# The next expert's gate products between an expert's up and down products, with its weights by whole rows and all programs written out

## The reference

```python
def ec_moe(h, lp):
    probs = jax.nn.softmax((xf @ lp["w_router"]).astype(jnp.float32), axis=-1)
    cap = CAPACITY_FACTOR * n // N_EXPERTS
    gate_vals, tok_idx = lax.top_k(probs.T, cap)
    xe = jnp.take(xf, tok_idx, axis=0)
    hid = jax.nn.silu(jnp.einsum("ecd,edf->ecf", xe, lp["w_e_gate"])) * jnp.einsum("ecd,edf->ecf", xe, lp["w_e_up"])
    ye = jnp.einsum("ecf,efd->ecd", hid, lp["w_e_down"]) * gate_vals[..., None].astype(h.dtype)
    y = jnp.zeros_like(xf).at[tok_idx.reshape(-1)].add(ye.reshape(-1, D))
```

## Time and profile before

| | us |
|---|---|
| median of 3 runs | 1850.94 |
| lowest and highest | 1848.95, 1852.34 |
| the profiled execution's own time | 1852.01 |
| its span | 1850.0 |
| PE busy | 1727.9 (93%) |
| DVE, ScalarE, GpSimd busy | 376.0, 185.5, 135.6 |

### The profile page before, as it was taken

How to read it: one execution, slowest core, us unless ns; L and a number is a source line. 1 busy time by engine, 2 the same in 40 slices (tenths; PEclk the granted TensorE clock), 3 DMA queues, 4 the chain that set the end, 5 groups by cost and what they waited for, 6 DMA issues and landing times.

```text
span 1850.0 us, 43144 instructions
## 1 busy us (share of the span) xinstructions
PE 1727.9 (93%) x19754; PEld 805.4 (44%) x19754; DVE 376.0 (20%) x695; ACT 185.5 (10%) x295; POOL 135.6 (7%) x204
## 2 busy tenths in 40 slices
PE   6999899799989999989999989998999899999997
PEld 3787568443434343434343434343434343434342
DVE  4422643611010101010101010101010101010103
ACT  4432431200000000000000000000000000000011
POOL 1000010120000000000001010000010101010000
PEclk9999959799999999999999999999999999999999
DMA  8521723999999999999999999999999999999991
GB/s 295 205 74 48 261 84 132 359 399 416 410 402 413 381 401 370 400 372 399 373 399 373 400 372 404 369 403 367 404 368 402 368 402 372 401 373 400 372 372 79
DMA packets 123373, 628.73 MB, mean 340 GB/s; under 512 B 11198, under 2 KB 14099, under 8 KB 106795
## 3 DMA queue, kind: packets, MB, share of 16 engines
q1 hardware_dynamic: 111872, 598.74, 81.9%
q0 software_dynamic: 10256, 23.91, 4.4%
q10 hardware_dynamic: 1050, 2.97, 0.4%
HBM read 609.37 MB, written 16.21 MB: 338 GB/s over the span
## 4 chain that ended last, share of the span: by engine, by line
PE 91%; issue 4%; DVE 2%; DMA 2%; ACT 1%; ACTq 0%; DVEq 0%; POOLq 0%
PE bank L1780 51%; PE bank L1792 16%; PE bank L1794 8%; PE bank L1369 3%; PE bank L1370 3%; PE bank L1371 3%; PE bank L1621 1%; PE bank L1396 1%; PE bank L1617 1%; PE bank L1679 1%; DMA raw<-in_w_out 0%; PE bank L1391 0%; DMA pos_col<-in_pos 0%; DMA xg<-xn_dram,idxG 0%; DVE S L1093 0%
## 5 line engine op out<-in xcount | busy, mean ns | idle before, releaser
L1780 PE MATMUL bank<-ring,xe 128*32 128x352 f32 x12288 | 943.6, 471 | 67.3 <-issue 64.0
L1780 PEld LDWEIGHTS bank<-ring,xe 128*32 128x32 f32 x12288 | 389.2, 113 | 619.4 <-issue 615.0
L1792 PE MATMUL bank<-ring,hidT 128*32 128x512 f32 x2816 | 364.5, 592 | 0.0
L1300 DVE TENSOR_TENSOR hid<-sg,bank 128x1056 f32<-128x1056 f32 x32 | 40.1, 1254 | 921.3 <-PE bank L1780 921.3
L1794 PE MATMUL bank<-ring,hidT 128*32 128x256 f32 x2816 | 214.5, 379 | 0.0
L1794 PEld LDWEIGHTS bank<-ring,hidT 128*32 128x32 f32 x2816 | 87.5, 110 | 214.7 <-issue 214.7
L881 ACT ACT_TABLE_LOAD x16 | 20.5, 1283 | 962.0 <-PE bank L1780 962.0
L1792 PEld LDWEIGHTS bank<-ring,hidT 128*32 128x32 f32 x2816 | 87.5, 110 | 67.0 <-issue 5.5
L643 POOL DMA_INDIRECT acc_dram<-yab,idx_s x15 | 24.3, 1622 | 1137.2 <-DVE yc L1311 1137.2
L1309 DVE SCALAR_TENSOR_TENSOR yab<-bank,gate_cur,gfab 128x512 f32<-128x512 f32 x16 | 12.0, 751 | 329.9 <-PE bank L1794 329.9
L881 ACT ACTIVATE sg<-bank 128x1056 f32<-128x1056 f32 x32 | 33.6, 1051 | 417.3 <-PE bank L1780 417.1
(11 more groups left out here) (262 smaller groups left out, 817.5 us busy)
## 6 DMA issues: line engine op xcount, KB each, us to landing
ring<-in_w_e_gate SPq DMA_DIRECT2D x128, 1408.0 KB, 9.2
ring<-in_w_e_up SPq DMA_DIRECT2D x128, 1408.0 KB, 8.9
ring<-in_w_e_down SPq DMA_DIRECT2D x96, 1536.0 KB, 9.3
ring<-in_w_e_down SPq DMA_DIRECT2D x32, 1024.0 KB, 8.5
raw<-in_w_ada SPq DMA_DIRECT2D x16, 1024.0 KB, 6.5
raw<-in_w_in SPq DMA_DIRECT2D x8, 1024.0 KB, 5.5
ada_f<-in_w_ada SPq DMA_DIRECT2D x4, 1024.0 KB, 16.7
raw<-in_w_out SPq DMA_DIRECT2D x4, 1024.0 KB, 8.8
```

The costliest lines, as they stand in the source:

```text
L1300: nc.vector.tensor_tensor(hid[:, :, :], sg[:, :, :], psum[:, 3:3 + ROW_TILES, 0:GCOLS], ALU.mult).then_inc(hid_done, 1)
L1780: last = nc.tensor.matmul(bank[b][32 * g:32 * g + 32, 0:GCOLS], xe[:, t, c, :], w[:, n, GCOLS * g:GCOLS * g + GCOLS], start=c == 0, stop=c ...
L1792: nc.tensor.matmul(bank[6][r:r + 32, :], hidT[:, ph, t, c, :], w[:, n, 512 * h:512 * h + 512], start=first, stop=stop)
```

## The change

- **Order on PE.** gate(0); then for each expert e: up(e), gate(e + 1), down(e). Gate and up both use banks 0 to 5, six banks of 352 columns, for all 2816 columns (`PHASES` is gone). A gate bank waits for DVE's product of the expert before (`hid_done`), an up bank for ScalarE's SiLU (`silu_done`).
- **Weights.** Ring of 13 slots of 2816 numbers. A gate or up load is one whole row for each partition (1408 KB, rows of 11264 bytes); a down load is two rows of 1024 (1024 KB). 27 loads an expert.
- **ScalarE and DVE** work bank by bank: six SiLUs and six products of 352 columns. The product is written over `sg`. `xe` has two buffers. DVE's order for each i: `weigh(i - 1)`, `rows_in(i + 1)`, `activated(i)`.
- **Context's down products.** Two chunks at a time go into the two halves of bank 7's partitions, 512 columns wide, as two partial sums. Both are weighed and added to `acc_dram`.
- **GpSimd.** Three scatters for each expert instead of two: `yab` with 128 rows of 2 KB, then each half of `yc` with 64 rows of 2 KB. Each is waited for before the next. The copies of row numbers are gone.
- **Programs.** All loops are written out, on all engines.

The diff, cut to its core:

```diff
@@ expert_units @@
+    order = [("gate", 0, q) for q in range(CH)]
+    for e in range(EXPERTS):
+        order += [("up", e, q) for q in range(CH)]
+        if e + 1 < EXPERTS:
+            order += [("gate", e + 1, q) for q in range(CH)]
+        order += [("down", e, q) for q in range(DOWN_UNITS)]
@@ SP @@
-            with sp.Fori(0, EXPERTS - 1) as i:
-                for j in range(EXP_UNITS):
-                    sp.wait_ge(unit_used, unit(j - RING + EXP_UNITS, i) + 1)
-                    expert_load(j, i, 1)
+            for n in range(len(UNITS)):
+                if n < RING:
+                    fill(n)
+                else:
+                    sp.wait_ge(unit_used, used(n - RING))
+                load(ring_unit(n), ring_source(n), ring_full[ring_slot(n)])
@@ GpSimd @@
             def rows_of(i):
-                for t in range(ROW_TILES):
-                    pool.wait_ge(xg_in[t], 16 * i + 16)
                 pool.wait_ge(xe_t, 3 * i + 3)
-                nc.gpsimd.tensor_copy(idx_g[:, :], idxG[:, bass.ds(3 * i + 3, 3)]).then_inc(pool_step, 1)
...
                 for t in range(ROW_TILES):
-                    gather(t, idx_g[:, t:t + 1])
+                    gather(t, idxG[:, 3 * i + 3 + t:3 * i + 4 + t])
...
-                pool.wait_ge(y_done, 2 * i + 4)
-                for a, y in ((0, yab), (1, yc)):
+                pool.wait_ge(y_done, 2 * i + 2)
+                for a, y, r in ((0, yab, slice(0, P)), (1, yc, slice(0, 64)), (1, yc, slice(64, P))):
                     nc.gpsimd.indirect_dma_start(
...
+                    n_s[0] += 16
+                    pool.wait_ge(scattered, n_s[0])
                 pool.sem_inc(y_free, 1)
@@ DVE @@
+            def activated(i):
+                for b in range(BANKS):
+                    t, h = divmod(b, HALVES)
+                    dve.wait_ge(silu_done, BANKS * i + b + 1)
...
+                    nc.vector.tensor_tensor(part_, part_, bank[b][:, 0:GCOLS], ALU.mult).then_inc(hid_done, 1)
...
+            for i in range(EXPERTS):
+                if i >= 1:
+                    weigh(i - 1)
+                if i + 1 < EXPERTS:
+                    rows_in(i + 1)
+                activated(i)
+            weigh(EXPERTS - 1)
@@ PE @@
+            def gate(e):
+                def begin(b):
+                    if e >= 1:
+                        pe.wait_ge(hid_done, BANKS * (e - 1) + b + 1)
+                    if b % HALVES == 0:
+                        pe.wait_ge(xe_done, 3 * e + b // HALVES + 1)
...
+                    for a in range(2):
+                        for h in range(2):
+                            r = 64 * a + 32 * h
+                            last = nc.tensor.matmul(bank[7][r:r + 32, :], hidT[:, 2, 2 * q + a, :], w[:, a, 512 * h:512 * h + 512], start=first, stop=stop)
...
+            gate(0)
+            pe.wait_ge(idx_sb, 4)
+            for e in range(EXPERTS):
+                up(e)
+                if e + 1 < EXPERTS:
+                    gate(e + 1)
+                down(e)
```

More of the change, by code:

```diff
@@ L128, in expert_units, with ring_slot, last_in @@
 def expert_units():
[L130 to L142, removed]
+    order = [("gate", 0, q) for q in range(CH)]
[4 more added lines that the diff above has]
+        order += [("down", e, q) for q in range(DOWN_UNITS)]
+    return order
+UNITS = expert_units()
+PLACE = {u: n for n, u in enumerate(UNITS)}
+TAIL_SLOTS = (9, 10, 11)
+def ring_slot(n):
+    return EXP_SLOTS[n % RING]
+def last_in(slots):
+    return max(n for n in range(len(UNITS)) if ring_slot(n) in slots)
 def state_slot(t, c, direction, start):
@@ L616, in _ @@
             for q in range(4):
[L617 removed]
+                step(nc.gpsimd.memset(iota[32 * q:32 * q + 32, 1, 0:1], float(q % 2)))
             w = 1
@@ L1308, in weigh @@
+            def weigh(i):
+                last = i == EXPERTS - 1
+                dve.wait_ge(unit_used, used(PLACE["down", i, DOWN_UNITS - 1]))
                 dve.wait_ge(y_free, i + 1)
-                nc.vector.scalar_tensor_tensor(out=yab[:, :], in0=bank[6][:, :], scalar=gate_cur[:, 0:1], in1=gfab[:, :], op0=ALU.mult, op1=ALU.mult).then_inc(y_done, 1)
+                nc.vector.scalar_tensor_tensor(out=yab[:, :], in0=bank[6][:, :], scalar=gateW[:, 2 * i:2 * i + 1], in1=gfab[:, :], op0=ALU.mult, op1=ALU.mult).then_inc(y_done, 1)
@@ L1797, in expert @@
-            def expert(i, first):
-                if first:
-                    for t in range(ROW_TILES):
-                        pe.wait_ge(xe_done, t + 1)
-                        for j in range(4):
-                            if t == 0:
-                                loaded(j, i)
-                            last = into(j, t)
+                        k = (HALVES * g + h) * GCOLS
+                        last = nc.tensor.matmul(bank[b][32 * g:32 * g + 32, 0:GCOLS], xe[:, e % 2, t, c, :], w[:, 0, k:k + GCOLS], start=c == 0, stop=c == CH - 1)
@@ new lines, in into @@
+                    if c == CH - 1 and b < BANKS - 1:
+                        last.then_inc(acc_ps, 1)
+                return last
+            def gate(e):
[4 more added lines that the diff above has]
+                        pe.wait_ge(xe_done, 3 * e + b // HALVES + 1)
+                ns = [PLACE["gate", e, c] for c in range(CH)]
+                if e == 0:
+                    for t in range(ROW_TILES):
+                        for n in ns:
+                            loaded(n)
+                            last = into(n, t, begin)
@@ new lines, in up, with begin, down @@
+            def up(e):
+                def begin(b):
+                    pe.wait_ge(silu_done, BANKS * e + b + 1)
+                for c in range(CH):
+                    n = PLACE["up", e, c]
+                    loaded(n)
+                    for t in range(ROW_TILES):
+                        last = into(n, t, begin)
+                    last.then_inc(unit_used, 1)
+            def down(e):
+                for q in range(DOWN_UNITS):
+                    n = PLACE["down", e, q]
+                    w = ring_unit(n)
@@ L1821, in expert @@
-                    if kind == "down":
-                        down(j, i)
-                        continue
-                    for t in range(ROW_TILES):
-                        if j == 0:
-                            pe.wait_ge(xe_done, 3 * i + t + 1)
-                        last = into(j, t)
-                    last.then_inc(unit_used, 1)
-            expert(0, True)
-            with pe.Fori(1, EXPERTS) as i:
-                expert(i, False)
+                        pe.wait_ge(hT_done, BANKS * e + ROW_TILES)
```

266 lines of the change are left out of this document (117 added, 149 removed).

## The result

| | kernel before | changed kernel |
|---|---|---|
| median, us | 1851.64 | 1969.88 |
| lowest and highest, us | 1848.95, 1857.96 | 1968.54, 1972.76 |
| profiled execution: time, span, us | 1852.01, 1850.0 | 1972.76, 1970.9 |

The changed kernel is slower: ratio 1.0645, interval 1.0627 to 1.0664, or 118 us. The direction and the mechanism were forecast, the size was not: 63 us were predicted, and the time lies just outside the range.

What follows compares the result with a forecast made beforehand. TensorE was taken to bind, with DMA engines as full. Span 1850.0 less 95 for loops, plus 157 for 14 waits with their clock, plus 1.2, gave 1913.2, so a median of 1914 us; range 1840 to 1968.

Steps and rivals of the forecast that it cites:

- What bounds the kernel: Expert stage before: TensorE busy 93% of the span, DMA engines as full; an expert costs 92.1 us for 85.35 of work.
- the loop's credit: PE's expert loop: writing it out removes 14 jumps of 6.8 us each, 95 us less.
- The wait that decides: PE ahead of gate(e+1), 14 times: idle 9.0 us for gathered rows and banks emptied by DVE.
- the sum: Chain from the end of down(e-1): weighing, three scatters, gathers, DVE; 37.5 us, where PE is ready at 28.5.
- rival (a): Scatter and gather chain hidden behind up(e), PE not waiting: 1756 us, or 1767 once DMA engines bind; chance 0.09.
- The clock behind the wait: PE after each idle time: the clock drops to half speed, costing another 2.2 us.
- Weights by whole rows ... I take no change: Weight loads in longer rows: rates of 415 and 421 GB/s, no change; bound some 1 us an expert either way.
- the scatters: GpSimd's three serial scatters in the chain: 9.5 us for the first, 7.0 each for the second and third.
- the scatters' landings as ends of a range: Scatters of 7.9, 5.9, 5.9 up to 10.4, 9.9, 9.9 us: with the gather, chain of 31 to 46 us.
- the prediction's signs: If right: about 14 PE waits at gate products, released by DVE, 6 to 13 us; scatters 6 to 10 us apart.
- the missing gate: Behind expert 15 no gate follows, so the wait comes only for e = 1 to 14.
- Head and tail: Small DVE operations on the tables and four last weighings of 512 columns: +1.2 us in all.

Runs made afterwards that it cites:

- the early gather: Changed kernel with GpSimd gathering the rows of expert e+1 ahead of the scatters of expert e-1 instead of behind them: 1756.7 us, ratio 0.9496.
- half rows: Changed kernel with each weight load issued as two of half rows (5632 or 4096 bytes for each partition), same bytes and order: 1918.23 us.

## Why the prediction was right or wrong

- **What bounds the kernel, and the loop's credit: right.** 95 us were credited; written-out loops alone gave 1850.4 - 1757.1 = 93 us.
- **The wait that decides: right** in place, number and releaser: 14 waits at the gate products behind `sg`, the chain in the order of the sum. Gathering first removes all of them; the 1756 us that rival (a) gave for a hidden chain, before DMA binds, is what that kernel takes. The rival's final figure, 1767 with DMA as the bound, was too high: PE waited there for no load, at 415 GB/s.
- **The clock behind the wait: right.** A gate stretch behind a wait takes 31.14 - 28.59 = 2.55 us more at expert 3. By PE's timeline it is 1.3 to 2.9 us at the 14 places, 29.3 us together, or 2.1 for each wait, where 2.2 were taken.
- **"Weights by whole rows ... I take no change": this is the step that failed.** It asked only what whole rows do to the rate of the weight loads, and there it was right (404 GB/s during up(3), and 415 with the early gather). It did not ask what they do to the other DMAs in the same engines, GpSimd's scatters. These were costed from the earlier trace rows, which were measured with rows of 5632 bytes in the weight queue. With such rows the sum nearly holds: 9.5 us of idle time measured, 9.0 predicted. The terms that were mis-sized are the scatters: 11.0, 8.2 and 8.2 in place of 9.5, 7.0 and 7.0, which is 3.9 of the 4.2 us by which the average wait (13.2) exceeds 9.0. That is 14 x 4.2 = 59 us. Of the 4.2, the runs put 2.9 on the length of the rows and 0.8 on loads of twice the size and half the number, or on the spread between single executions. With half rows 0.5 are left, and there each scatter of 64 rows, which the prediction took from between two bounds, landed in 7.5 and not 7.0. That half rows land within 4 us of 1914 is partly luck, since two terms named below, +3.3 at the end and -4 at the start, nearly cancel.
- **Taking the scatters' landings as ends of a range: too narrow for the same reason.** The longest landing in the trace, 10.4 us, was taken as the upper end of `yab`; the median became 11.0. An end read from a trace holds only as long as the queues carry the same load. The same shows in the prediction's signs: it named waits of 6 to 13 us and 6 to 10 us between scatters; the waits were 11.9 to 14.6, and from the first scatter to the second it was 11.1 on average.
- **Missed altogether: 3.3 us ahead of the last down products.** Between up(e) and down(e) lies gate(e + 1), which hides product and transposes; behind expert 15 there is none. The prediction named the missing gate only as a reason for 14 waits. The line in PE's timeline of the changed kernel:

```profile
1923.13 1.92 PE L1836 MATMUL bank<-ring,hidT 128*32 128x512 f32 x16 [3.33 <-DVE hidT L1305]
```

- **Head and tail:** the tail is about 1 us longer, about as said. But the first expert matmul starts at 366.4 in the changed kernel and at 370.2 in the profiled execution before. The cause stays open. It is not in the expert stage: a small matmul for the tables of row numbers, the same in both, already starts at 358.7 against 362.6, and the kernel before with its loops written out starts its experts at 365.3 too.

The account of the spans, predicted 1913.2, measured 1970.9: +58 for the waits and their clock, +3.3 for the last down products, -3.8 at the start. That the last two nearly cancel is luck.

## What to carry to other kernels

When a consumer is moved forward, follow back what feeds it and move that too: here the gather stayed behind three serial scatters that it did not depend on, and moving it was worth 213 us. A change to the shape of bulk loads is to be priced twice, for their own rate (25 us here) and for the latency of the small DMAs that share the engines (46 us); a latency read from a trace holds only for the traffic that it was measured in. Before crediting a large rewrite, run its smallest part alone: written-out loops alone gave all of the gain that the mended change has.

## What the runs showed of the hardware that I had not expected

- **The rows of one queue set the latency of another's scatter.** Landing of 128 rows added in place: 8.2, 9.1 and 11.0 us with 2816, 5632 and 11264 bytes for a row of the weight loads, at the same bytes loaded. The 4.8 us up to the first row stay; the passage of the rows shrinks from 5.1 to 3.6 and 2.6 us, with 1.1 to 1.5 weight rows for each scattered row. The traces do not say on which DMA engine a packet ran, so the turns on one engine are inferred from these counts.
- **A jump of the long loop comes with a fetch of instructions.** PE was idle 4.3 to 4.8 us at each of 14 jumps, with one packet of 16 KB of the instruction queue inside each pause, and 93 us went with the jumps.
- **DMA share does not tell the rate.** Shares of 1.01 and 1.02 stood beside 415, 404 and 252 GB/s: whole rows, half rows in twice the loads, and halves of the partitions.
- **Short rows in many loads cost a little rate when the engines are the bound,** 404 against 415 GB/s. Whole rows in as many loads keep 415, so it is the length of the rows. The kernel before with its loops written out, which has half rows of gate and up in undivided loads, ran at 407 with small pauses; what the rows of gate and up and what those of down add was not measured apart.
